# A two-block network on one core: pieces, window means, decay rows, attention steps and joins put into other half units

## The reference

```python
# block 1
h = rmsnorm(x) * (1 + scale_m) + shift_m            # shift, scale, gate: silu(c) @ w_ada, 6 x 1024 columns
z, xbc, dt, u_pool, gates = split(h @ w_in)
y  = ssd_scan(silu(conv4(xbc)), dt) * silu(z)       # state-space scan: 4 groups x 4 chunks of 128 tokens
yp = (mean over the last 2/4/8/16 tokens of u_pool - u_pool) @ pool_w        # sliding means
x += gate_m * ((g_ssd * (norm(y) @ w_ssd) + g_pool * (yp @ w_pool)) @ w_out)
x += gate_f * (relu(h2 @ w_up)**2 @ w_down);  x = rmsnorm(x)
# block 2
qk, v, o, gates, q_at, kv_at = split(h @ w_in_2)
m  = mlstm(silu(conv4(qk)), v, gates);  m = rms_norm(m) * sigmoid(o)   # gate recurrence: cumsum, cummax
a  = rms_norm(window_attention(rope(q_at), rope(k_at), v_at))          # 8 heads, window 128
x += g1 * rms_norm(concat(m, a) @ w_out_2)
x += g2 * rms_norm(conv_ffn(h2))
```

## Time and profile before

| | us |
|---|---|
| median of 3 runs | 1857.09 (1852.63 to 1859.3) |
| the profiled execution | 1854.17, its span 1852.4 |
| TensorE busy | 1681.6 (91% of the span) |
| VectorE, GpSimd, ScalarE busy | 884.6, 796.4, 634.1 |
| mean granted TensorE clock | 0.949 of full speed |

### The profile page before, as it was taken

The page is one execution under the profiler, slowest core; times in us unless marked ns, Lnnn a source line. Parts: engine busy times, 40 slices in busy tenths (PEclk is TensorE's granted clock), DMA queues, the critical chain, the costliest instruction groups (busy, mean ns, idle before and its releaser), DMA issues.

```text
span 1852.4 us, 20603 instructions
## 1 busy us (share of the span) xinstructions
PE 1681.6 (91%) x7578; PEld 1351.5 (73%) x7578; DVE 884.6 (48%) x1165; ACT 634.1 (34%) x824; POOL 796.4 (43%) x636
## 2 busy tenths in 40 slices
PE   3988999999899999799999997989857799999995
PEld 2666778787688877588888886768746477888784
DVE  5536454555645352643344455564744755113324
ACT  3434434343223222432133222444123444334421
POOL 1263545555344544345545552313243255444441
PEclk7889999999899999899999997979979899999998
DMA  8111112122135534145544441211011033222221
GB/s 315 46 68 44 71 69 91 69 69 91 68 113 183 182 136 159 68 147 180 189 149 143 170 182 55 85 46 60 33 46 68 23 136 108 94 105 91 85 94 60
DMA packets 35234, 194.32 MB, mean 105 GB/s; under 512 B 3904, under 2 KB 4160, under 8 KB 19776
## 3 DMA queue, kind: packets, MB, share of 16 engines
q1 hardware_dynamic: 23616, 151.06, 22.7%
q10 hardware_dynamic: 11520, 41.95, 6.5%
...
## 4 chain that ended last, share of the span: by engine, by line
PE 72%; DVE 14%; POOL 5%; ACT 4%; issue 3%; DMA 2%; DVEq 0%; SPq 0%; ACTq 0%; POOLq 0%
PE main L727 56%; PE main L723 8%; POOL w_lo L573 5%; ACT w_hi L1027 2%; DVE rstd L1624 1%; PE auxB L751 1%; DMA raw<-stream 1%; DVE h_lo L1654 1%; PE auxD L830 1%; DMA ada_first<-w_ada 1%; DVE tmp L1419 1%; PE auxD L895 1%; DVE tmp L1562 1%; DVE x L1639 1%; DVE ysum L1638 1%
## 5 line engine op out<-in xcount | busy, mean ns | idle before, releaser
L573 POOL TENSOR_TENSOR w_lo<-raw,w_hi 128x512 fp32r<-128x512 f32 (+1 forms) x522 | 703.5, 1379 | 854.8 <-ACT w_hi L1027 854.5
L727 PE MATMUL main<-h_hi,w_hi 128*128 128x512 f32 (+2 forms) x1136 | 458.5, 404 | 38.5 <-DVE h_lo L1654 16.4
L727 PE MATMUL main<-h_lo,w_hi 128*128 128x512 f32 (+2 forms) x1136 | 449.8, 396 | 0.0
L727 PE MATMUL main<-h_hi,w_lo 128*128 128x512 f32 (+2 forms) x1136 | 449.5, 396 | 0.0
L1027 ACT ACTIVATE w_hi<-raw 128x2048 fp32r<-128x2048 f32 (+3 forms) x136 | 247.9, 1823 | 269.9 <-PE main L727 230.5
L727 PEld LDWEIGHTS main<-h_hi,w_hi 128*128 128x128 f32 (+2 forms) x1136 | 216.0, 190 | 106.6 <-issue 25.7
L727 PEld LDWEIGHTS main<-h_hi,w_lo 128*128 128x128 f32 (+2 forms) x1136 | 216.1, 190 | 48.8 <-issue 1.0
L727 PEld LDWEIGHTS main<-h_lo,w_hi 128*128 128x128 f32 (+2 forms) x1136 | 216.6, 191 | 44.1 <-issue 0.5
L1562 DVE SCALAR_TENSOR_TENSOR tmp<-main,par,tmp 128x511 f32<-128x511 f32 x88 | 65.9, 749 | 176.3 <-ACT tmp L1128 174.7
L1587 DVE SCALAR_TENSOR_TENSOR ada_acc<-ada_raw,cs,ada_acc 128x1024 f32<-128x1024 f32 x70 | 114.3, 1634 | 29.4 <-DMA ada_raw<-w_ada 20.8
L723 PE MATMUL main<-w_hi,h_hi 128*128 128x512 f32 (+1 forms) x256 | 101.7, 397 | 19.8 <-POOL w_lo L573 10.2
...
## 6 DMA issues: line engine op xcount, KB each, us to landing
...
```

What stands on the lines that cost most here:

```text
L573: ins = nc.gpsimd.tensor_tensor(w_lo[:, s, a:b], raw[:, s, a:b], w_hi[:, s, a:b], ALU.subtract)
L727: ins = nc.tensor.matmul(bank[0:n, :], w[:, k, col:col + n], a[:, ka_, :], start=start, stop=stop)
```

## The change

Steps move to other half units, and three of them are cut in two; the products, norms and transfers stay the same, but for the two points marked with a star.

1. **Pieces.** The 24 pieces of `w_ada` that lay two by two in GS0 to BP2 now lie two by two in GS0 to GS3 and GP0 to GP2, one each in PW, GP3 and BP0 to BP3, and two each in OUT0 and OUT1. `ada_sum` moves from the end of a unit to the middle of the next one (but where the next one is UP0, KV or FU0).
2. **Decay rows.** GpSimd's part of `seg_rows` becomes `seg_fill` in the middle of BC, behind `split_lo` of Z0 and ahead of that of Z1.
3. **Sliding means.** Each window comes two half units later; `p_lo` of a window is made at the start of the next one (`window_lo`), the last in `window_last`. *The copies of the first columns are replaced by one running sum over the first 2 to 16 columns.
4. **Gate recurrence.** `ml_scan` from the end of QK0 to its middle, `ml_exp` from the middle of QK1 to the end of QK0, `ml_columns` from the end to the middle of QK1.
5. **Attention.** All stages two half units later: scores from the middle of QK1 to the end of V0, the last `att_out` in the middle of O0.
6. **Joining.** The attention half gets its own step `att_join` (TensorE turns, VectorE scales) from the middle of O0 to the end of O1, and `att_hi` ahead of WO (ScalarE rounds, GpSimd takes the rest). The gates of the heads (`heads`) move to the end of O1. `join` keeps the cell's half; *its `h_lo` is made by VectorE in place of GpSimd. WO multiplies rows 4 to 7 (attention) first, and waits for rows 0 to 3 only then.
7. **Norm 3.** The four steps of squares that lay in the middle of WO0 become three there and one in the middle of WO1, with the norm behind it (it was at the end of WO0); the squares of norm 4 move into the middle of WO2.

```diff
-    slots = [n for n in range(gs0, gs0 + 12) for s in both]
+    slots = [n for n in range(gs0, gs0 + 4) for s in both] + [gs0 + 4]
+    slots += [n for n in range(gs0 + 5, gs0 + 8) for s in both] + [gs0 + 8]
+    slots += [n for n in range(gs0 + 9, gs0 + 13)] + [n for n in range(gs0 + 13, gs0 + 15) for s in both]
+    mid[find("BC")] += [("seg_fill", 0)]
-        slot(2 * at["U"][0] + 1 + n).append(("window", t))
+        slot(2 * at["U"][0] + 3 + n).append(("window", t))
+    slot(2 * at["U"][0] + 3 + KD).append(("window_last", 0))
-    end[at["QK"][0]] += [("rope_q", 2), ("rope_q", 3), ("ml_scan", 0)]
-    mid[at["QK"][1]] += [("ml_exp", 0)]
-    end[at["QK"][1]] += [("ml_columns", 0)]
+    mid[at["QK"][0]] += [("ml_scan", 0)]
+    end[at["QK"][0]] += [("rope_q", 2), ("rope_q", 3), ("ml_exp", 0)]
+    mid[at["QK"][1]] += [("ml_columns", 0)]
-    first = 2 * at["QK"][0]
+    first = 2 * at["QK"][1]
+        slot(first + 10 + i).append(("att_join", i))
-    before[at["WO"][0]] += [("join", c) for c in range(TC)]
+    end[at["O1"][0]] += [("heads", 0)]
+    before[at["WO"][0]] += [("att_hi", 0)] + [("join", c) for c in range(TC)] + [("join_last", 0)]
-    mid[wo] += all_sums(3)
-    end[wo] += [("norm", 3)]
-    end[wo + 1] += [("sumsq", (4, 0))]
-    mid[wo + 2] += [("sumsq", (4, 1))]
+    mid[wo] += all_sums(3)[:-1]
+    mid[wo + 1] += [all_sums(3)[-1], ("norm", 3)]
+    mid[wo + 2] += [("sumsq", (4, 0)), ("sumsq", (4, 1))]
-            end[n].append(("ada_sum", p // 8 + 2))
+            (end[n] if n + 1 in ada_due else mid[n + 1]).append(("ada_sum", p // 8 + 2))
...
+                    if u.name == "WO":
+                        ks = (4, 5, 6, 7, 0, 1, 2, 3)
+                        if t == 0 and u.n == unit_at["WO"][0] and k in (0, 4):
+                            pe.wait_ge(*((ja_hi if k else jn_hi), TC))
+                            pe.wait_ge(*((ja_lo if k else jn_lo), TC))
...
+            def att_hi(i, n):
+                act.wait_ge(*units_over(unit_at["WO"][0]))
+                for c in range(TC):
+                    act.wait_ge(ja_t, c + 1)
+                    run_act(h_hi[:, 4:8, chunk(c)], att_t[c], ACT.Copy).then_inc(ja_hi, 1)
...
             def window(t, n):
-                    dve.wait_ge(pl_lo, n)
+                    window_lo(n - 1)
-                    nc.vector.tensor_copy(dst[:, 0:d], src[:, 0:d])
-                    link(tt(dst[:, d:SEQ], src[:, d:SEQ], src[:, 0:SEQ - d], ALU.add))
+                    whole += d
+                    link(tt(dst[:, whole:SEQ], src[:, whole:SEQ], src[:, whole - d:SEQ - d], ALU.add))
+                link(nc.vector.tensor_tensor_scan(src[:, 0:w], u[:, 0:w], nothing[:, 0:w], 0.0, ALU.add, ALU.add))
+            def heads(i, n):
+                for c in range(TC - 1):
+                    gate_heads(c)
+                finish_heads()
+                gate_heads(TC - 1)
+            def join_lo(c):
+                dve.wait_ge(jn_hi, c + 1)
+                tt(h_lo[:, 0:4, chunk(c)], tmp[:, c, :].rearrange("p (t d) -> p t d", t=4), h_hi[:, 0:4, chunk(c)],
+                   ALU.subtract).then_inc(jn_lo, 1)
```

More of the change, by code:

```diff
@@ L286 @@
             "att_scores": "BC", "att_turn": "BC", "att_out": "D", "ml_scores": "BC", "ml_out": "DBACAC",
-            "join": "AB"}
+            "att_join": "A"}
 SPREAD = (1, 2, 3, 4, 6)
@@ L310, in build @@
             banks = "D" if item == sum_stage(item[0]) else ""
+        elif name == "join":
+            banks = "AB"[item % 2]
         else:
@@ L486, in build @@
                  ("ysum", 3, None, "add"), ("x", 4, 9, "h"), ("ysum", 5, None, "add")]
-        eps_both, weight_both = small[:, 20:21], small[:, 24:32]
+        eps_both, weight_both, nothing = small[:, 20:21], small[:, 24:32], small[:, 36:52]
         NORM_EPS_OF = [pc("eps1"), pc("eps1"), eps_both, pc("eps1"), pc("eps2"), pc("eps2"), pc("eps2")]
@@ L953, in ml_out_, with att_join @@
                     ins.then_inc(full, 1)
-            def join(c, n):
-                bank, full = take(("join", c), 1)
+            def att_join(c, n):
+                bank, full = take(("att_join", c), 0)
                 pe.wait_ge(at_out, c + 1)
@@ L960, in join @@
                 ins.then_inc(full, 1)
+            def join(c, n):
                 bank, full = take(("join", c), 0)
@@ L969, in _ @@
                       "att_scores": att_scores, "att_turn": att_turn, "att_out": att_out_, "ml_columns": ml_columns,
-                      "k_turn": k_turn, "ml_scores": ml_scores, "ml_out": ml_out_, "join": join}
+                      "k_turn": k_turn, "ml_scores": ml_scores, "ml_out": ml_out_, "att_join": att_join,
+                      "join": join}
             count = {}
@@ L1347, in _ @@
                       "rope_k": rope_k, "rope_q": rope_q, "att_exp": att_exp, "att_turn": att_turn, "att_square": att_square,
-                      "ml_gates": ml_gates, "ml_exp": ml_exp, "k_turn": k_turn, "ml_scores": ml_scores, "join": join}
+                      "ml_gates": ml_gates, "ml_exp": ml_exp, "k_turn": k_turn, "ml_scores": ml_scores, "att_hi": att_hi, "join": join}
             count = {}
@@ L1927, in _ @@
                       "ssd_scores": ssd_scores, "ssd_out": ssd_out, "ssd_turn": ssd_turn, "window": window,
-                      "att_scores": att_scores, "att_out": att_out, "att_norm": att_norm, "ml_gates": ml_gates,
+                      "window_last": window_last, "att_scores": att_scores, "att_out": att_out, "att_norm": att_norm, "ml_gates": ml_gates,
                       "ml_scan": ml_scan, "ml_columns": ml_columns,
-                      "ml_scores": ml_scores, "ml_out": ml_out_, "join": join}
+                      "ml_scores": ml_scores, "ml_out": ml_out_, "att_join": att_join, "heads": heads,
+                      "join": join, "join_last": join_last}
             count = {}
@@ L1947, in _ @@
             ts(mn_half, pc("ml_norm"), 0.5, None, ALU.mult)
+            nc.vector.memset(nothing, 0.0)
             nc.vector.memset(eps_both, NORM_EPS * RMS_EPS)
```

84 lines of the change are left out of this document (45 added, 39 removed).

## The result

The changed kernel takes 1831.4 us (median of 4 runs, 1824.7 to 1834.3) beside 1858.1 of the kernel before (4 runs, 1852.6 to 1859.3): a ratio of 0.986 with a 95% interval of 0.983 to 0.989. The forecast was 1821, with 1808 to 1838 around it. In the profiled executions the span went from 1852.4 to 1828.1 us, 24.3 less, where the terms of the sum promised 36.

A forecast was written before the change was run, and what follows sets the result against it. TensorE, busy 1681.6 of 1852.4 us, was taken as the bound, with waits and slow clock to recover. Terms 6 + 8 + 3 + 4 + 8 + 7 = 36 us off 1857.1 gave 1821 us, range 1808 to 1838.

The forecast's parts named there:

- the first rival: V0 to O1: moved attention steps come on top of the recurrence's, gates start late; 1835 us, chance 0.18.
- Decay rows, 6 us: Z0 and Z1: w_lo of Z0 no longer waits behind GpSimd's fill; 6 us gained, bounds 3.3 and 7.3.
- just in time: Z1: w_lo ready at 115.4 for a turn at 116.0, down to 2 us late if Z0 runs at full clock.
- Sliding means, 8 us: U, Y0 and Y1: later windows free the weights, a 3 to 5 us stall stays; 8 us gained, bounds 4 and 12.
- Pieces, 3 us: BP and OUT: 5.5 gained at BP2, 1 on ada_sum's waits, 3.5 lost at OUT; 3 us, bounds -4 and +7.
- Shared DMA engines: OUT: a piece's transfer costs the full 1.3 us; with separate queues it would cost nothing and the sum were 4.
- Recurrence and attention, 4 us: QK to O1: 8 us gained by QK1's end, 4 given back in V1 and O0; bounds -6 and +9.
- Joining, 8 us: O1 to WO0: TensorE reaches WO0 after 9.5 us in place of 18.0; 8 us gained, bounds 4 and 11.
- Norm 3, 7 us: WO0 to WO2: the 8.0 us wait becomes 2.6 in WO1; 7 us gained, bounds 4 and 9.
- the moved attention is repaid: V0 and O0: if VectorE ends each half unit, attention and recurrence go from +4 to -6; 1835 us, chance 0.18.
- the clock comes back more: Z0, U, BP, QK, WO: every stall removed takes its slow stretch with it; 48 us, 1809 us, chance 0.11.

The follow-up runs named there:

- c1_all: Changed kernel with means in middle steps ended by GS0, att_join last, no pieces in OUT0 and OUT1, VectorE making attention's h_lo: 1819.6 us, ratio 0.979.
- a2: Changed kernel with att_join behind ml_out and ml_scores in each half unit of V1 and O: 1828.8 us, ratio 0.984 to the kernel before.
- a3: Changed kernel with the four pieces of OUT0 and OUT1 moved to PW, GP3, OUT2 and OUT3: 1824.1 us, ratio 0.982 to the kernel before.
- a4: Changed kernel with VectorE in place of GpSimd making h_lo of the attention half: 1830.0 us, ratio 0.985 to the kernel before.
- a1: Changed kernel with one sliding mean in the middle step of each of eight units, none at a unit's end: 1824.8 us, ratio 0.981.

## Experiments: what held the change back

### The means again

After the change ScalarE makes `w_hi` right behind a window five times in a row, for the fourth U unit to GS1, as this part of its timeline shows for Y0, Y1 and GS0 (idle time before in brackets). The release of each `p_hi` is VectorE's window. TensorE waits four times for the `w_lo` that comes of it, 9.2 us in all, up to 3.4 (ahead of the fourth U unit, Y0, Y1 and GS0; the expectation below names the third U unit too, which is one too many), where it waited twice for 8.6 before.

```profile
498.42 0.63 ACT L1287 ACTIVATE p_hi<-tmp 128x512 fp32r<-128x512 f32 x1 [4.63 <-DVEq L1783]
498.96 1.90 ACT L1041 ACTIVATE w_hi<-raw 128x2048 fp32r<-128x2048 f32 x1
...
511.61 0.63 ACT L1287 ACTIVATE p_hi<-tmp 128x512 fp32r<-128x512 f32 x1 [2.44 <-DVEq L1783]
512.15 1.90 ACT L1041 ACTIVATE w_hi<-raw 128x2048 fp32r<-128x2048 f32 x1
...
525.22 0.63 ACT L1287 ACTIVATE p_hi<-tmp 128x512 fp32r<-128x512 f32 x1 [4.17 <-DVEq L1783]
525.75 1.91 ACT L1041 ACTIVATE w_hi<-raw 128x2048 fp32r<-128x2048 f32 x1
```

```profile
PE main L738 <- POOL w_lo L583: 9.2, 4, 3.4
```

In the program ScalarE rounds the weights of unit n+2 directly behind the end steps of unit n; its middle steps are over half a unit earlier. Two windows of 16, one behind the other, also show what a `w_lo` beside them costs: 0.19 and 0.18 us for the small steps in the first, 1.13 and 1.17 in the second. GpSimd's row stands last.

```profile
497.14 0.19 DVE L1779 TENSOR_TENSOR_SCAN tmp<-xs_tok,small 128x16 f32<-128x16 f32 x1
497.36 0.18 DVE L1780 TENSOR_TENSOR tmp<-tmp,con 128x16 f32<-128x16 f32 x1
...
500.73 4.06 DVE L1776 TENSOR_TENSOR tmp<-tmp 128x509 f32<-128x509 f32 x3
504.82 1.13 DVE L1779 TENSOR_TENSOR_SCAN tmp<-xs_tok,small 128x16 f32<-128x16 f32 x1
505.99 1.17 DVE L1780 TENSOR_TENSOR tmp<-tmp,con 128x16 f32<-128x16 f32 x1
...
500.94 6.19 POOL L583 TENSOR_TENSOR w_lo<-raw,w_hi 128x512 fp32r<-128x512 f32 x4 [9.18 <-ACT w_hi L1041]
```

So there were two suspects: the windows ahead of `w_hi` in ScalarE's queue, and VectorE held by GpSimd. This edit takes the windows from the ends of the units and leaves them beside the `w_lo`. With it there is one window in a unit and no longer two:

```diff
-        slot(2 * at["U"][0] + 3 + n).append(("window", t))
-    slot(2 * at["U"][0] + 3 + KD).append(("window_last", 0))
+        mid[at["U"][0] + 1 + n].append(("window", t))
+    mid[at["U"][0] + 1 + KD].append(("window_last", 0))
```

> The changed kernel, with one sliding mean in the middle step of each of eight units (from the second U unit to GS2) and none at a unit's end. From the first U unit to GS0 the change takes 79.6 us for 65.4 us of matmuls, and TensorE waits for w_lo before the third and fourth U unit, Y0, Y1 and GS0. Theory 1: each of these waits stands because ScalarE makes w_hi of the unit after next only behind the mean of a unit's end. Without one there the waits go: the stretch shrinks by 8 to 11 us, up to 2 of which may come back under GS0 to GS3, where the means now stand beside the pieces; 7 to 10 us faster than the change. Theory 2 (the cost is VectorE held beside GpSimd's w_lo, wherever the means stand): the stretch shrinks by under 3 us.

```profile
452.90:520.80 67.90, 67.90 (x305) 55.52 (x304) 40.34 (x55) 20.46 (x23) 33.33 (x24) 1.00 0.27 96
520.80:570.80 50.00, 46.96 (x194) 37.97 (x193) 31.88 (x37) 13.69 (x15) 23.20 (x16) 0.93 0.41 144
```

67.9 us for the stage, 11.7 less, TensorE busy all of it at full clock: the windows ahead of `w_hi` were the cost. Theory 2 falls. How much of it is the slot and how much the wider spacing, this edit does not separate; c1_all, below, with two windows in one middle step, shows that the spacing counts too. But 5.6 came back from GS0 to PW, more than the 2 expected: in the middle of GS1 a window stands ahead of two pieces, ScalarE's issue of the next pieces behind them and `w_hi` behind that. It starts at 548.52, 5.9 us after GS2's first matmul, and TensorE waits 3.0 us, with a slow half unit behind.

```profile
545.19 0.63 ACT L1287 ACTIVATE p_hi<-tmp 128x512 fp32r<-128x512 f32 x1 [7.22 <-DVEq L1783]
...
546.63 1.78 ACTq L1165 DMA_DIRECT2D ada_raw<-w_ada  x2
548.52 1.92 ACT L1041 ACTIVATE w_hi<-raw 128x2048 fp32r<-128x2048 f32 x1 [2.21 <-DVEq L1609]
```

### Pieces in OUT

VectorE's timeline of the change in OUT0 and OUT1, then ScalarE's: the pieces wait behind the eviction that waits 9.29 us for x, ScalarE's issue and `w_hi` wait behind the pieces, 12.45 us.

```profile
692.15 0.75 DVE L1521 SCALAR_TENSOR_TENSOR x<-main,mul,x 128x512 f32<-128x512 f32 x1 [9.29 <-DMA x<-x_in]
693.15 2.72 DVE L1603 SCALAR_TENSOR_TENSOR ada_acc<-ada_raw,cs,ada_acc 128x1024 f32<-128x1024 f32 x2 [0.25 <-DVE x L1521]
```

```profile
694.53 1.77 ACTq L1165 DMA_DIRECT2D ada_raw<-w_ada  x2
696.39 1.92 ACT L1041 ACTIVATE w_hi<-raw 128x2048 fp32r<-128x2048 f32 x1 [12.45 <-DVEq L1609]
```

```diff
-    slots = [n for n in range(gs0, gs0 + 4) for s in both] + [gs0 + 4]
-    slots += [n for n in range(gs0 + 5, gs0 + 8) for s in both] + [gs0 + 8]
-    slots += [n for n in range(gs0 + 9, gs0 + 13)] + [n for n in range(gs0 + 13, gs0 + 15) for s in both]
+    slots = [n for n in range(gs0, gs0 + 9) for s in both]
+    slots += [n for n in range(gs0 + 9, gs0 + 13)] + [gs0 + 15, gs0 + 16]
```

> The changed kernel, with the four pieces of OUT0 and OUT1 moved: one more each in PW and GP3, one each in OUT2 and OUT3. Theory 1: in the change w_hi of OUT1 and OUT2 stand on ScalarE behind pieces of VectorE that stand behind the eviction which waits 9.3 us for the reload of x; with no piece before OUT2 the wait of 2.9 us before OUT2, the slow 7.4 us half unit and the second wait in it go: the first UP unit starts 5 to 6 us earlier than in the change, less up to 2 us that the second piece costs at GP3 and PW. Theory 2: the transfer of OUT's weights, with the DMA engines 0.97 busy, is late by itself: under 2 us.

OUT takes 56.7 us in place of 62.0, and the second pieces in PW and GP3 cost nothing: 5.3 us, and theory 1. `w_hi` now starts 13.5 us after OUT0 instead of 15.6, released by the transfer itself:

```profile
693.20 1.92 ACT L1040 ACTIVATE w_hi<-raw 128x2048 fp32r<-128x2048 f32 x1 [10.41 <-DMA raw<-stream]
```

The rest is the `w_lo` behind it, 5.49 us here and 7.41 in the change, beside the pieces of OUT1.

### The order in V1 to O1

```diff
-            "att_scores", "k_turn", "att_join", "ml_out", "ml_scores"]
+            "att_scores", "k_turn", "ml_out", "ml_scores", "att_join"]
```

> The changed kernel, with att_join behind ml_out and ml_scores in each half unit of V1 and O, in place of ahead of them. V0 to O1's end takes 97.5 us there. Theory 1: att_join takes bank A first, so that ml_out waits for VectorE's scaling of it (0.8 to 1.2 us) behind 0.6 us of turning, four times; behind the recurrence's chain only the 0.6 stay, and with less rest the slow first half units of V1 and O0 (7.3 us for 5.7) may go: 5 to 9 us less. Theory 2: VectorE's chain alone sets the pace, the order does not matter: under 2 us.

94.9 us, which is 1.0 below the lowest and 3.9 below the highest of the kernels with the old order, and short of the 5 to 9 of theory 1. TensorE's pauses and small products in V0 to O1 add up to 49.6 us in the change and 50.2 here; what differs is how many half units ran slow, two there and none here. c1_all, below, has this order too and takes 96.7, with two slow half units: a gain by the order is not shown.

### GpSimd beside the gates

The change's joining: three gates in 4.78 us, a scaling in 1.75, then a gate in 0.69, once GpSimd's four subtractions (1338.3 to 1344.6, the last two rows) are through.

```profile
1338.69 4.78 DVE L1936 SCALAR_TENSOR_TENSOR hm<-og,hm 128x512 f32<-128x512 f32 x3 [0.25 <-DVE prob_t L1930]
1343.39 1.75 DVE L1926 TENSOR_TENSOR hm<-hm,small 128x512 f32<-128x512 f32 x1
1345.17 0.69 DVE L1936 SCALAR_TENSOR_TENSOR hm<-og,hm 128x512 f32<-128x512 f32 x1
...
1338.27 2.95 POOL L641 TENSOR_TENSOR h_lo<-prob,h_hi 128x512 fp32r<-128x512 f32 x2 [0.52 <-ACT h_hi L1355]
1341.18 3.41 POOL L641 TENSOR_TENSOR h_lo<-prob_t,h_hi 128x512 fp32r<-128x512 f32 x2
```

```diff
             def att_hi(i, n):
                 for c in range(TC):
-                    pool.wait_ge(ja_hi, c + 1)
-                    nc.gpsimd.tensor_tensor(h_lo[:, 4:8, chunk(c)], att_t[c], h_hi[:, 4:8, chunk(c)],
-                                            ALU.subtract).then_inc(ja_lo, 1)
+                    pass
...
                 dve.sem_inc(jn_t, 1)
+                if c == 1:
+                    dve.wait_ge(*units_over(unit_at["WO"][0]))
+                    for a in range(TC):
+                        dve.wait_ge(ja_hi, a + 1)
+                        tt(h_lo[:, 4:8, chunk(a)], att_t[a], h_hi[:, 4:8, chunk(a)], ALU.subtract).then_inc(ja_lo, 1)
                 if c:
                     join_lo(c - 1)
```

> The changed kernel, with VectorE making h_lo of the attention half between the scalings of the second and third head turn, in place of GpSimd beside the gates. O1's end to WO0 takes 11.6 us there. Theory 1: beside GpSimd's four subtractions three gates took 4.78 us for 2.1 unhindered, and a scaling 1.74 for 0.69; without them these 3.7 us go, and four subtractions of 0.69 come: 9.0 to 10.0 us, 2 us less. Theory 2: the gates are slow by themselves: WO0 starts 2.8 us later, 14.4 us.

```profile
1343.50 1.90 DVE L1934 SCALAR_TENSOR_TENSOR hm<-og,hm 128x512 f32<-128x512 f32 x3 [0.24 <-DVE prob_t L1928]
1345.31 0.68 DVE L1924 TENSOR_TENSOR hm<-hm,small 128x512 f32<-128x512 f32 x1
```

1.90 us for the same three gates and 0.68 for the scaling, 3.95 us less, and WO0 starts 9.7 us after O1's end instead of 11.6: theory 1. The median does not show the 2 us; QK ran 3.2 us longer in its profiled execution with the same steps.
The Trainium skill, "SBUF — State Buffer", section "SBUF: two separate sides", says that of a VectorE instruction with two SBUF inputs and a GpSimd one that reads SBUF, the one that starts first has the shared port for its whole length and the other blocks. The rows agree: under the subtractions of 1.3 to 1.7 us each, a gate takes 1.6 us on the mean instead of 0.69, and a step of 16 columns beside `w_lo` takes 1.1 to 1.2 us instead of 0.17 to 0.19.

### All together

```diff
+        mid[at["U"][0] + (1, 2, 3, 4, 4, 5, 5, 6)[n]].append(("window", t))
+    mid[at["U"][0] + 7].append(("window_last", 0))
```

with the edits of a2, a3 and a4 (the diff shows how the means differ from a1).

> The changed kernel with four edits together: sliding means in middle steps only, ended by GS0 (two each in Y0 and Y1, where VectorE has little to do, none from GS1 on, where the first form lost 6 us again); att_join last; no pieces in OUT0 and OUT1; VectorE making h_lo of the attention half. If the gains add: 10 to 12 us by GS0 and none given back, 5 in OUT, 4 in V1 to O1, 2 at the joining: 20 to 23 us less than the change, a span of 1805 to 1809 us and a ratio of 0.973 to 0.976 to the kernel before. Rival: with TensorE ahead, ScalarE's and VectorE's queues become the limit in the same stages, and half of it stays: 1815 to 1819.

1819.6 us, a ratio of 0.979, and a span of 1818.9: near the rival's. The pairs of means were the mistake: `w_hi` of GS0 and of GS1 came late behind the second mean of each, TensorE waited 1.8 and 2.7 us, and the first half unit of GS1 took 8.6 us. The next kernel separates them again:

```diff
+    slots = [gs0, gs0, gs0 + 1, gs0 + 2] + [n for n in range(gs0 + 3, gs0 + 9) for s in both]
+    slots += [n for n in range(gs0 + 9, gs0 + 13)] + [gs0 + 14, gs0 + 15, gs0 + 15, gs0 + 16]
```

with the means of a1 and VectorE's `h_lo` of a4.

> The four-edit kernel once more, with no pair of means in one half unit: one each in the middle of eight units, as in the first form; to make room for them GS1 and GS2 have one piece instead of two, and OUT1 and OUT2 one more each; att_join back ahead of ml_out, since its place made no difference to TensorE's gaps. Theory (w_hi of GS0 and GS1 was late behind the second mean of a pair, w_hi of GS3 behind a mean and two pieces): by GS0 12 us are gained on the change, as in the first form, of the 5.8 lost again by PW 1.5 to 3 stay lost, OUT gives 4 to 5, the joining 2: 15 to 18 us under the change's span of 1828.1, that is 1810 to 1813, and a ratio of 0.974 to 0.977. Rival: one piece in GS1 still makes w_hi of GS3 late, and a stall of any length costs the same slow half unit behind it: 4 to 6 stay lost, 1814 to 1817.

1816.5 us (5 runs, 1816.0 to 1819.0), a ratio of 0.979 (0.978 to 0.981), and a span of 1814.6, 13.5 less than the change's. U to GS0 is at 67.9 again, OUT at 57.2, the joining at 9.7. From GS0 to OUT0 4.8 us more than in the change stayed lost, the rival's size, and by half of its mechanism. They are three waits of some 1.5 us each. The first two, at the ends of GS2 and GS3, are for `w_lo`: `w_hi` of GS3 stood behind a window and one piece, as the rival had it, and that of PW behind the same. The third, at PW's end, is for VectorE, whose evictions of PW (L1498) stood behind two pieces. But no half unit ran slow behind them, which the rival had wrong. Its median and span are the lowest of all kernels run here, 2.1% below the one before; by the ratio it is level with c1_all.

## Why the prediction was right, and where it was not

- **The whole.** Right in direction and range, 10 us too hopeful: 24 to 27 us came of 36. By the stages of the two traces the six terms gave 4.6, 2.0, 1.6, 3.8, 6.4 and 6.5, where they stood at 6, 8, 3, 4, 8 and 7, so more than half of what is missing is the sliding means. The measured 1831.4 lies above the forecast's own 1812 to 1830; the wider range, which takes in the first rival (1835), holds it. (Taken as independent, the terms' bounds give 1812 to 1835, and not 1830.)
- **Decay rows, 6 us.** Right: 6.0 undone alone, 4.0 to 6.8 over all kernels. The clock I hoped to get back in Z0's first half is a draw that can fall either way; `w_lo` of Z1 was "just in time", as told.
- **Sliding means, 8 us: the step that failed.** The move gave 2 us, and a gain by the scan is not shown. What failed is the sentence that the rest of the windows lies under Y0 and Y1, "whose weights have slack once TensorE has stalled for 3". The stall before the fourth U unit came as forecast (3.5 us). But the `w_hi` of Y0, Y1 and GS0 stood behind the window at the end of the unit two before each, so there was no slack: the two stalls were traded for four smaller ones (9.2 us for 8.6). One window in the middle of each unit gave 11.7 us, nearly all of the stall and slow clock that was there.
- **Pieces, 3 us.** Between the traces the three stages give 1.6. With the products of `ada_sum` (1.7) put where they were, GS to BP give 6.1, where I had 6.5, and OUT takes 4.5, where I had 3.5. The mechanism at OUT was the one told; what I left out was that the pieces of OUT1 stretch the `w_lo` beside them from 5.5 to 7.4 us, and that a slow half unit follows the stall.
- **Shared DMA engines.** The rule of the Trainium skill, "DMA: Bandwidth & Descriptors", section "Issuing engines are not separate DMA queues", weighed 1.3 us in the prediction; no run here separates it from the wait for VectorE, which was the larger.
- **Recurrence and attention, 4 us.** 3.8 by the traces (20.3 gained, 16.5 given back), but from two errors that cancel: the shift is worth 9.1 and not 5, all of it pauses; and three of the `att_join` cost up to 6.8 and not 1, of it 1.8 for 3 x 0.6 us of turning, another 1.8 of pauses, for the most part waits for VectorE's scaling of bank A, and 3.2 of slow half units that may be a draw. That the term came out at 3.8 is luck.
- **Joining, 8 us.** 6.4, since TensorE reached WO0 after 11.6 us instead of 9.5. The gates held by GpSimd stood in the bound and not in the sum; they are 3.95 us of VectorE's time with the scaling. WO0 did start ahead of the last `join_lo`, as forecast.
- **Norm 3, 7 us.** Right: 6.5 by the traces, 7.2 undone alone. The wait left over was 4.0 us and not 2.6.
- Of the rivals, "the moved attention is repaid" named the place where most was given back, but the shift still paid; "the clock comes back more" was wrong: nearly each stage kept a slow half unit.

The parts undone alone add up to more than the whole: 6.0 + 2 + 2.5 + 9.4 + 9.1 + 7.2, about 36 us, and 43 with the 6.4 of the joining, for 24.3 in the spans. Up to 6.8 us of the difference are `att_join`, which none of these undoes. Another 7 or so are half units that ran slow in the kernel with a part undone and at full pace in the change or before (PW 2.9, DN0 1.6, Y0 and GS0 2.5). How far the rest is one part standing in for another, no run separates. So a term measured by undoing it once carries the draws of that execution, and they all look like gains of the change.
